# One shared product per level of a bidirectional linear-attention scan, decay logits over eight slabs, and a new first stage

## The reference

```
logits = (h @ w_a1) @ w_a2 + b_a ;  log_decay = log_sigmoid(logits) / 16
cum    = cumsum(log_decay) inside a chunk
attn[t, s] = sum_d q[t, d] * k[s, d] * exp(cum[t, d] - cum[s, d])      for s <= t
out    = attn @ v + (q * exp(cum)) @ state
state  = exp(last) * state + (k * exp(last - cum))^T @ v
```

## Time and profile before

| what | value |
|---|---|
| median of 3 runs | 1894.07 us |
| the profiled execution: its own time, its span | 1895.03 us, 1892.1 us |
| PE busy | 1721.5 us (91%) |
| DVE busy | 1181.0 us (62%) |
| ACT busy | 711.5 us (38%) |
| POOL busy | 258.1 us (14%) |
| L395, one of three products per tile, 128x512 and 128x256 | 1600 times, 356 ns on average |
| mean granted TensorE clock of the span | 0.95 |

### The profile page before, as it was taken

One profiled execution on the slowest core, in us unless ns is written; L12 is line 12 of the kernel. 1 busy time (PEld: TensorE's weight loads), 2 busy tenths in 40 slices (PEclk: granted clock), 3 DMA queues, 4 the chain that ended last, 5 costly groups with the idle time before them and its releaser, 6 DMA issues.

```text
span 1892.1 us, 24788 instructions
## 1 busy us (share of the span) xinstructions
PE 1721.5 (91%) x9208; PEld 1474.1 (78%) x9208; DVE 1181.0 (62%) x1781; ACT 711.5 (38%) x1030; POOL 258.1 (14%) x214
## 2 busy tenths in 40 slices
PE   5999789987999999999997899967778799999996
PEld 5888677876888888888886678857767678888875
DVE  6688566578886587757757531277873655365465
ACT  2211555325442223223345632433432445343344
POOL 2300000123000000000024000066761300000002
PEclk9999999988999999999997889988888899999998
DMA  8244000121334333333220112200002132332321
GB/s 350 89 150 156 34 1 1 56 100 56 101 132 134 123 118 115 133 132 124 67 81 23 45 48 64 97 1 1 1 12 68 56 91 98 101 95 94 100 89 67
DMA packets 37422, 161.01 MB, mean 85 GB/s; under 512 B 4160, under 2 KB 4416, under 8 KB 31072
## 3 DMA queue, kind: packets, MB, share of 16 engines
q1 hardware_dynamic: 37344, 159.94, 25.2%
HBM read 157.83 MB, written 2.10 MB: 85 GB/s over the span
## 4 chain that ended last, share of the span: by engine, by line
PE 77%; DVE 11%; issue 4%; ACT 4%; POOL 2%; DMA 1%; DVEq 0%; ACTq 0%; SPq 0%; POOLq 0%
PE pm L395 59%; PE pm L415 5%; PE pm L580 3%; PE pm L686 2%; DVE row L1272 1%; PE pm L704 1%; DVE fade L1530 1%; DVE pairs L1591 1%; PE pm L427 1%; DVE probs L1295 1%; PE pm L436 1%; PE pm L456 1%; PE pm L516 1%; ACT probs L860 1%; POOL both_b L1685 1%
## 5 line engine op out<-in xcount | busy, mean ns | idle before, releaser
L1138 DVE TENSOR_TENSOR w_lo<-raw,w_hi 128x1024 fp32r<-128x1024 f32 x193 | 243.3, 1261 | 431.4 <-ACT w_hi L797 428.7
L395 PE MATMUL pm<-x_hi,w_hi 128*128 128x512 f32 x1600 | 474.1, 356 | 13.7 <-DVE acc_g L1443 10.6
L395 PE MATMUL pm<-x_lo,w_hi 128*128 128x512 f32 x1600 | 471.7, 354 | 0.0
L395 PE MATMUL pm<-x_hi,w_lo 128*128 128x512 f32 x1600 | 471.6, 354 | 0.0
L797 ACT ACTIVATE w_hi<-raw 128x1024 fp32r<-128x1024 f32 x191 | 202.4, 1059 | 673.9 <-PE pm L395 606.0
L395 PEld LDWEIGHTS pm<-x_hi,w_hi 128*128 128x128 f32 x1600 | 262.4, 190 | 63.6 <-issue 16.3
L395 PEld LDWEIGHTS pm<-x_hi,w_lo 128*128 128x128 f32 x1600 | 262.0, 190 | 43.5
L395 PEld LDWEIGHTS pm<-x_lo,w_hi 128*128 128x128 f32 x1600 | 261.6, 190 | 43.3
L1645 POOL TENSOR_TENSOR sum<-sum,sq_t 128x768 f32<-128x768 f32 (+1 forms) x32 | 53.1, 1660 | 979.9 <-ACT sq_t L897 979.9
L395 PE MATMUL pm<-hid_hi,w_hi 128*128 128x512 f32 (+1 forms) x396 | 119.6, 356 | 1.4 <-DVE w_lo L1138 1.4
L395 PE MATMUL pm<-hid_hi,w_lo 128*128 128x512 f32 (+1 forms) x396 | 119.9, 357 | 0.0
(11 more groups left out here) (196 smaller groups left out, 2605.2 us busy)
## 6 DMA issues: line engine op xcount, KB each, us to landing
raw<-slabs SPq DMA_DIRECT2D x193, 512.0 KB, 3.6
ada_w<-ada SPq DMA_DIRECT2D x44, 1024.0 KB, 4.9
ada_w<-first_ada SPq DMA_DIRECT2D x4, 1024.0 KB, 20.0
h_res<-x SPq DMA_DIRECT2D x4, 768.0 KB, 18.3
out<-h_res SPq DMA_DIRECT2D x8, 256.0 KB, 2.0
cond_rep<-cond_rep SPq DMA_DIRECT2D x1, 1024.0 KB, 5.6
level_f<-level SPq DMA_DIRECT2D x1, 896.0 KB, 4.9
rope<-rope SPq DMA_DIRECT2D x1, 512.0 KB, 22.5
```

What stands on the lines that cost most here:

```text
L395: last = pe.matmul(out_p[:, a:b], w[slot][:, ks], x[:, k, a:b], start=(k == 0 and w is w_hi and x is hi), stop=(k == tiles - 1 and w is w_lo))
L1138: dve.tensor_tensor(w_lo[nxt % 2][:, :], raw[nxt % 4][:, :], w_hi[nxt % 2][:, :].bitcast(FP32), ALU.subtract).then_inc(sem["split_lo"], 1)
```

## The change

- **Scan.** A level takes both directions at once. `sides(m)` (three buffers of 2 x 512) holds the key side in row 0 and the query side in row 1, for both directions: DVE writes four differences of 256, ACT takes Exp over all 1024 columns, DVE (not POOL) multiplies the rows with keys and queries, PE multiplies row 0 with row 1, and DVE copies with one mask that holds both directions' pairs. 7 levels a head in the place of 14. The places of the other work move to the new level numbers.
- **Decays of keys and queries.** `key_diff` and `query_diff` go; ACT works from `cum` with a bias per chunk (`chunk_sum` scaled by 1/16), so five and four activations of 128 columns in the place of one. POOL leaves out chunks that aren't used.
- **Logits.** The query slabs come right behind the key slabs, and two logits follow every second of the eight slabs.
- **First stage.** `cond_rep` is loaded on one partition (8 KB) and spread by four PE products; ACT modulates from `h_res` and takes the high part, DVE takes the low part; shift results go tile by tile over four banks. Slabs 0 and 1 are loaded with the first piece, 2 and 3 after the last.

```diff
-            sp.dma_start(cond_rep[:, :, :], rep_in).then_inc(sem["rep_in"], 16)
+            sp.dma_start(cond_rep[0:1, :, :], rep_in).then_inc(sem["rep_in"], 16)
...
-                slab_load(m, m)
+                if m == 0:
+                    slab_load(0, 0)
+                    slab_load(1, 1)
+            slab_load(2, 2)
+            slab_load(3, 3)
...
+            for c in range(2):
+                for a in (0, 512):
+                    last = pe.matmul(pm[c][:, a:a + 512], ones[0:1, 0:1].to_broadcast([1, P]), cond_rep[0:1, c, a:a + 512],
+                                     start=True, stop=True)
+                last.then_inc(sem["rep_spread"], 1)
...
-            for n in range(GLA_HEADS):
+            for n in range(2 * GLA_HEADS):
                 if n >= 1:
-                    slab(S_GLA, 0, n + 1, x_hi, x_lo, TOK)
-                logits(2 * n)
-                logits(2 * n + 1)
+                    slab(S_GLA, 0, n + 1, x_hi, x_lo, TOK if n < GLA_HEADS else LAT)
+                if n % 2 == 0:
+                    logits(n)
+                    logits(n + 1)
...
-                    if h >= 1 and lv in (1, 2, 3, 4):
-                        head_output(h - 1, (lv - 1,))
-                    if lv == 5:
+                    if h >= 1 and lv in (1, 2):
+                        head_output(h - 1, (2 * lv - 2, 2 * lv - 1))
+                    if lv == 3:
                         turn_keys(2 * h)
-                    if h >= 1 and lv == 7:
+                    if h >= 1 and lv == 4:
                         head_sums(h - 1)
-                    if h >= 1 and lv == 8:
+                    if h >= 1 and lv == 5:
                         head_spread(h - 1)
-                    if lv == 10:
+                    if lv == 6:
                         chunk_states(2 * h)
-                    if lv == 11:
                         turn_keys(2 * h + 1)
-                    if lv == 13:
+                    if lv == 7:
                         chunk_states(2 * h + 1)
...
             for n in range(KT):
+                act.wait_ge(sem["ada_taken"], n + 1)
+                act.wait_ge(x_loaded[n // 2], 16)
+                if n >= 4:
+                    act.wait_ge(sem["x_ready"], n - 3)
+                for c, (a, b) in enumerate(HALVES):
+                    last = act.activation(mod_t[:, n % 4, a:b], h_res[:, n, a:b], ACT.Identity,
+                                          bias=mods[:, 0, SH1 + n, c:c + 1], scale=mods[:, 0, SC1 + n, c:c + 1])
+                last.then_inc(sem["mod_f"], 1)
                 high_part(n, 0, TOK)
...
+                if q >= 1:
+                    act.wait_ge(sem["k_turned"], q)
                 if q % 2 == 0:
-                    act.wait_ge(sem["k_diff"], h + 1)
-                    src = k_out[:, :]
+                    for c in SCAN[0]:
+                        cs = slice(c * P, (c + 1) * P)
+                        last = act.activation(k_out[:, cs], cum[:, 0, h, cs], ACT.Exp, bias=chunk_sum[:, 0, h, c:c + 1], scale=-INV)
...
-                for lv in range(LEVELS - 1):
-                    m = (LEVELS - 1) * h + lv
+                for b in range(GLA_LEVELS):
+                    m = GLA_LEVELS * h + b
                     act.wait_ge(sem["diff_done"], m + 1)
-                    act.activation(fade[:, m % 4, :], fade[:, m % 4, :], ACT.Exp, scale=INV).then_inc(sem["fade_done"], 1)
-                    if lv == 1:
+                    act.activation(sides(m)[:, :, :], sides(m)[:, :, :], ACT.Exp, scale=INV).then_inc(sem["fade_done"], 1)
+                    if b == 0:
                         diagonal(h)
-                    if h >= 1 and lv == 6:
+                    if h >= 1 and b == 2:
                         square_output(h - 1)
-                    if lv == 7:
+                    if b == 3:
                         copy_keys(2 * h)
+                    if b == 4:
+                        if h >= 1:
+                            output_std(h - 1)
                         key_decay(2 * h + 1)
...
+                    if h >= 1 and b == 5:
                         copy_rms(h - 1)
-                    if lv == 10:
+                    if b == 6:
                         query_decay(h)
-                    if lv == 12:
                         copy_keys(2 * h + 1)
                 if h + 1 < GLA_HEADS:
                     key_decay(2 * h + 2)
...
+            for m in range(KT // 2):
+                for half in range(2):
+                    first_scale(m, half)
+                    if m > 0:
+                        first_low(2 * m - 2 + half)
+                if m == 0:
+                    for s in range(2):
+                        rest(s, s)
+                for half in range(2):
+                    take_first(2 * m + half)
...
+                for z in range(2):
+                    left, right, mid = segments(b, z, h)
+                    to_left, _, _ = segments(b, z, h, sides(m)[:, z, :])
+                    _, to_right, _ = segments(b, z, h, sides(m)[:, 1 - z, :])
+                    dve.tensor_tensor(to_left, mid, left, ALU.subtract)
+                    last = dve.tensor_tensor(to_right, right, mid, ALU.subtract)
+                last.then_inc(sem["diff_done"], 1)
+
+            def level_sides(m):
+                if m >= GLA_HEADS * GLA_LEVELS:
+                    return
+                h = m // GLA_LEVELS
+                dve.wait_ge(sem["fade_done"], m + 1)
+                dve.tensor_tensor(sides(m)[:, 0, :], sides(m)[:, 0, :], gla_k[:, h, 0:LAT], ALU.mult)
+                dve.tensor_tensor(sides(m)[:, 1, :], sides(m)[:, 1, :], gla_q[:, h, :], ALU.mult).then_inc(
+                    sem["sides_done"], 1)
...
-            for m in range(3):
+            for m in range(2):
                 level_diff(m)
+            level_sides(0)
             for h in range(GLA_HEADS):
-                for lv in range(LEVELS - 1):
-                    level_diff((LEVELS - 1) * h + lv + 3)
-                    n = LEVELS * h + lv + 1
+                for b in range(GLA_LEVELS):
+                    m = GLA_LEVELS * h + b
+                    level_diff(m + 2)
+                    level_sides(m + 1)
+                    if h >= 1 and b == 4:
+                        output_rms(h - 1)
+                    if h >= 1 and b == 5:
+                        scale_output(h - 1)
+                    n = LEVELS * h + b + 1
                     dve.wait_ge(sem["gram_done"], n + 1)
                     dve.wait_ge(sem["level_used"], n)
...
+                    if b == 6:
                         scan(2 * h)
...
                 scan(2 * h + 1)
                 if h >= 1:
                     output_low(h - 1)
...
             fade_keys(0)
             for h in range(GLA_HEADS):
-                for lv in range(LEVELS - 1):
...
+                fade_keys(2 * h + 1)
+                if h >= 1:
+                    gate_output(h - 1)
+                fade_queries(h)
                 if h + 1 < GLA_HEADS:
                     fade_keys(2 * h + 2)
```

More of the change, by code:

```diff
@@ L260, in state_sum, with sides @@
             return (pm[1][:, 256 * j:256 * (j + 1)] if j < 4 else pm[3][:, 0:256])
-        def both(m):
-            return both_a[:, 0, :] if m % 3 == 2 else both_b[:, m % 3, :]
+        def sides(m):
+            return (sides0, sides1, sides2)[m % 3]
         def level_bank(n):
@@ L654, in _ @@
                 for u in range(4):
-                    slab(s_v, i, u, x_hi, x_lo, TOK)
+                    slab(S_GLA_V, i, u, x_hi, x_lo, TOK)
                     if u >= 1:
@@ L658, in _ @@
                 turn_v(3)
-            with pe.Fori(0, 3) as i:
+            with pe.Fori(0, 2) as i:
                 for u in range(4):
-                    slab(S_GLA + N_GLA_ALL, i, u, x_hi, x_lo, LAT)
+                    slab(S_GLA_G, i, u, x_hi, x_lo, LAT)
             pe.wait_ge(sem["psum_free"], S_GLA_OUT)
@@ L803, in _ @@
                 sem["cond_done"], 1)
-            act.wait_ge(sem["rep_in"], 16)
-            act.activation(cond_rep[:, :, :], cond_rep[:, :, :], ACT.Silu).then_inc(sem["rep_done"], 1)
+            for c in range(2):
+                act.wait_ge(sem["rep_spread"], c + 1)
+                act.activation(cond_rep[:, c, :], pm[c][:, :], ACT.Silu).then_inc(sem["rep_done"], 1)
+            for s in range(2):
+                split(s, s)
             def modulate(n, first, tokens, scale, shift):
@@ L988, in softplus, with take_query @@
                     act.activation(soft[:, j % 2, :], soft[:, j % 2, :], ACT.Ln, bias=1.0).then_inc(sem["log_done"], 1)
+            def take_query(s, i, u, src):
+                act.activation(gla_q[:, u - 1 - GLA_HEADS, :], src[:, 0:LAT], ACT.Copy, scale=P ** -0.5).then_inc(sem["psum_free"], 1)
             step(S_GLA, 0, 0, take_low)
-            for n in range(GLA_HEADS):
-                step(S_GLA, 0, n + 1, take_key)
-                softplus(n)
+            for n in range(2 * GLA_HEADS):
```

(46 more changed lines are left out.)

178 lines of the change are left out of this document (54 added, 124 removed).

## The result

The changed kernel took 1876.94 us (median of 7 runs, 1868.09 to 1881.78), the kernel before 1891.34 (7 runs beside it): a ratio of 0.991 with an interval of 0.9885 to 0.9936. The forecast was 1875. A second set of 7 gave 1880.15 against 1891.14, ratio 0.9934 (0.9906 to 0.9962). The total is near the forecast.

What follows compares the result with a forecast made beforehand. PE was taken as the bound except where it waits: first stage, logits and scan. Savings of 5.5 + 8.7 + 5.3 = 19.5 us from the profiled 1895.03 gave 1875.5, stated as 1875, range 1856 to 1889 (own range of the sum 1866 to 1886).

Steps and rivals of the forecast that it cites:

- First stage, 5.5: First stage: PE starts its tiles at 27.8, not 33.24, and ends at 58.3, not 63.7; 5.5 us saved (3 to 8).
- the two dots of 2.82 us: First stage: DVE is late partly because two dot products take 2.82 us, not 1.21, while POOL writes `x_lo`.
- Logits, 8.7: Logits stage: two slabs beside each pair of logits hide most of the chain of waits; 8.7 us saved (5 to 13).
- The low clock that I had put behind the pairs of logits: Logits stage: 1.7 us of lower clock charged to slab 4, as behind each pair of logits before.
- Scan, 5.3: Scan: head 0 and the end save time, two periods give some back; 5.3 us saved (-3 to +13).
- The ring: Scan: waits through DVE, ACT and PE around b = 6 set each head's period at 46 us (43 to 49), against 45.0.
- head 0 saves 4.1, two periods give 2.0 back, 3.2 saved at the end: Scan: first reciprocal 1299.4 against 1303.48, two periods of 46 us, 22.9 us after the last reciprocal against 26.1.
- DVE, 30 us a head: Scan: DVE's work is 7 x 3.2 + 4.9 + 3 = 30 us a head, under the 46 us period.
- which the prediction had put beside DVE's waits: Scan: only POOL's first key fade meets working DVE instructions, 1 us a head more; its other work meets DVE's waits.
- Rival B: Scan: the ring doesn't close, DVE is the bound, 36 us a head; 1848 us in all; chance 0.17.
- Rival D: Logits and first stage: ACT and DVE still serialise at every pair, scan brings nothing; 6 to 7 us saved, 1888; chance 0.14.
- Rival C: Scan: PE runs at 1.2 GHz, mean clock near 0.5, some 9 us a head more; 1898 us in all; chance 0.09.

Runs made afterwards that it cites:

- filling products: Identity products nobody reads, where TensorE waits in the scan: 48 a head added to the changed kernel, 1863.14 us; 34 a head added to the kernel before, 1877.53 us.
- the ring is open: Changed kernel with four moves in the scan's order of VectorE, TensorE and ScalarE work: 1842.59 us, ratio 0.9751 to the kernel before.
- one statement moved behind another: Changed kernel with VectorE's sides of the next head's first level moved behind the head's first scan: 1863.93 us, ratio 0.9858 to the kernel before.

## Why the prediction was right, and where it was not

**The total** agrees partly by luck. The forecast takes 19.5 us from 1895.03; the two ratios give 17 and 12.5 us from a median of 1891. In the two profiled executions the gain up to the start of the scan is 20.6 us where the forecast has 14.2, and the scan loses 2.4 up to the last head_output where it has 5.3 saved: a surplus of 6.4 has paid for a miss of 7.7. Over all traces the first two terms come to 15.7 (5.6 and 10.1), so most of that surplus is the spread between executions and not mechanism.

**First stage, 5.5.** Right in size: 4.2 by the run of this part alone (1.3 to 7.0), 5.6 by the mean of the traces. The first product starts at 28.43 against 27.8 forecast; the second shift came 0.8 late because its transfer did. Of the reasons given, one falls: the two dots of 2.82 us. With GpSimd's low parts back they return and the stage ends no later, because `w_lo` is now made ahead of them. What went is PE's wait of 4.24 us for `w_lo`; the second shift starts only 0.4 us earlier in these two traces.

**Logits, 8.7.** Right, slightly low: 9.8 and 10.1. The low clock that I had put behind the pairs of logits (1.7 us at slab 4) did not come. Counted from the first logits, the second pair is forecast at 21.4 us and starts at 19.6, the third at 39.9 and 36.5, the last single logit at 57.8 and 54.6. The stage ran at 0.97.

**Scan, 5.3.** Wrong: 5.1 slower alone, and 3.5, 3.9 and 5.1 longer in three traces with the whole change (the two of it and the one with the low parts on GpSimd). The ring was forecast well: 46 us, and 46.0 in the second period, though 48.4 in the first, and its chunk_states were priced at the low clock. From the end of scale_output over both chunk_states to the end of the second scan the forecast has 20.0 us (14.5 to 34.5), the trace 20.4 (1338.1 to 1358.5). The step that failed is "head 0 saves 4.1, two periods give 2.0 back, 3.2 saved at the end". From the first differences to the first reciprocal it is 61.5 us before and 61.8 after: nothing saved. The two periods gave 4.4 back, not 2.0. From the last reciprocal to the last product 32.4 became 31.2: 1.2 saved and not 3.2. Up to the begin of head_output, where the forecast's sum ends, it is 26.1 and 23.8, 2.3 saved; the other 1.1 are lost in head_output itself, 7.4 us in the place of 6.3, because more of its products run at the low level of the clock (0.63 us each, 0.39 at the high one).

These are 8.8 us, and the kernels with filling products tell what the clock has of them. With filling, the changed kernel's head 0 takes 59.6 us; the old one's stays at 61.5. So 2.2 of the 4.4 us missed in head 0 go with the clock. The two periods are 44.6 and 44.6 with filling and 48.4 and 46.0 without, the same instructions at two mean clocks (0.71 and 0.80 by head): the 2.4 us that the first has more than the second, which is the whole miss of the periods, are the clock too, and PE's rows above name them (3.41 for 1.84 us, 1.90 for 1.13). With the 1.1 of the last head_output that is 5.7 us. The other 2.2 of head 0 and 0.9 at the end were not taken apart.

I had weighed the clock as all or nothing, a rival with 9 us a head below a mean of 0.5, and written down no price for what lies between. It stood at 0.72 to 0.75. I had also taken the wrong measure of before: 45.0 us was its period at 0.84. With filling it is 41.7. Filled, the changed scan is still 2.4 us longer (174.9 against 172.5), but at 0.88 against 0.98, so which of the two is shorter at one clock stays open.

**DVE, 30 us a head.** It was 33.4 (66.73 in two heads). Three differences at b = 6 take 1.48 in the place of 0.42 beside POOL's gate and query fades (1337.55 to 1343.04), which the prediction had put beside DVE's waits. That costs nothing in the changed kernel, which waits for the Exp right behind them: the wait is 3.79 us, and not the 6 to 7 forecast, by just these 3.2. Once the ring is open and DVE is the bound, they should cost 3.2 us a head; that is an estimate from the durations, no run took them away.

**Rival B** (36 a head, 1848) described what the level loop is worth without the ring: 37.1 and 1842.6 when it was opened. **Rival D** is out, the logits had no wait for each pair. **Rival C** did not come in full (0.72 to 0.75, not 0.5), but its mechanism has 5.7 of the 8.8 us by which the scan missed.

What stays open: whether the parts help each other (8.9 against 12.5 to 17 us), what the 3.1 us of the scan are that the clock doesn't explain, and which scan is shorter at one clock.

## What to carry to other kernels

Halving the number of steps was worth nothing in this scan, whose engines wait for each other, until one edge of the ring of waits was cut. So write the ring out first; here one statement moved behind another was worth 10 to 14 us, nearly as much as the whole change. An order in which engine A asks for something that B does only after A's own next step shows in the trace as waits that come back at the same places of each period, and which one to cut is told by moving the later consumer, not by making the work faster. Where TensorE has gaps, take the price of the clock from the long and short durations of one and the same product in the trace, and count fewer products as a possible loss.

## What was not expected of the hardware

Products of no use made kernels faster: 48 a head (each 128x128 by 128x128 in float32) brought 15 to 17 us in the changed kernel, 34 a head 11.5 in the kernel before. The same ten chunk_states products take 4.61 us at the low level of the clock (1.2 GHz) and 2.32 at the high one (2.4 GHz), and in the changed kernel six of the eight groups, behind idle stretches of 2.7 to 7.7 us, took 4.08 or more. The Trainium skill, TensorE: Matmul & The Clock Gate (HAM oscillation), describes waits between bursts of products after which the next burst starts at the low clock, and these rows agree.

The exponential of 1024 columns took 1.05 us where one of 512 takes 0.63, and five of 128 columns with a bias each took 1.56, against 0.74 for one of 640 columns.
